# Final RMSNorm of a two-layer kernel: norm weight before the turn, token factor after it

## What is computed

```
def per_layer_embed(h, p_i, norm_w, w_gate, w_proj):
    gate = jax.nn.sigmoid(rmsnorm(h, norm_w) @ w_gate)
    return ((p_i @ w_proj) * gate).astype(h.dtype)
...
        h = h + per_layer_embed(h, p[i], ple_norm_w[i], ple_w_gate[i], ple_w_proj[i])
    return rmsnorm(h, final_norm_w)
```

## Time and profile before

| | |
|---|---|
| runs shown | 1607.35, 1607.68, 1607.53 us |
| the profiled execution's own time | 1606.47 us |
| its span in the trace | 1604.8 us |
| TensorE (PE) matmul busy | 1524.5 us, 95% of the span |
| VectorE (DVE) busy | 1189.6 us, 74% |
| ScalarE (ACT) busy | 718.6 us, 45% |
| mean granted TensorE clock | 0.967 |

### The profile page before, as it was taken

The page is one execution under the profiler, slowest core; times in us unless marked ns, Lnnn a source line. Parts: engine busy times, 40 slices in busy tenths (PEclk is TensorE's granted clock), DMA queues, the critical chain, the costliest instruction groups (busy, mean ns, idle before and its releaser), DMA issues.

```text
span 1604.8 us, 20223 instructions
## 1 busy us (share of the span) xinstructions
PE 1524.5 (95%) x7365; PEld 1239.3 (77%) x7365; DVE 1189.6 (74%) x1371; ACT 718.6 (45%) x1091; POOL 243.8 (15%) x244
## 2 busy tenths in 40 slices
PE   7988999999989999999999989999999999999996
PEld 6757777687667888888876769988888888888884
DVE  5687768678787989988898969955677666643356
ACT  4554454444644555134445342433365555532242
POOL 1154111020127400030075100000100000000000
PEclk9999999999999999999999976979999999999998
DMA  4334215144225334543436587932233333332221
GB/s 141 86 122 132 79 66 173 51 145 131 66 66 108 115 119 143 196 133 130 151 118 209 174 299 249 264 85 94 93 95 99 94 93 103 105 98 92 92 92 59
DMA packets 192234, 199.01 MB, mean 124 GB/s; under 512 B 47886, under 2 KB 178526, under 8 KB 188062
## 3 DMA queue, kind: packets, MB, share of 16 engines
q1 hardware_dynamic: 184510, 192.76, 37.8%
q10 hardware_dynamic: 7648, 5.25, 1.2%
HBM read 169.47 MB, written 28.51 MB: 123 GB/s over the span
## 4 chain that ended last, share of the span: by engine, by line
PE 74%; DVE 15%; issue 5%; DMA 3%; ACT 2%; SPq 1%; POOL 0%; DVEq 0%; ACTq 0%
PE ring L2093 21%; PE ring L2083 21%; PE ring L2084 21%; DVE w_lo L1462 2%; PE ring L2349 2%; PE pe_s L2369 2%; DVE cc L1584 1%; PE ring L2234 1%; PE pe_s L2359 1%; DMA w_raw<-in_ssd_w_out 1%; DVE ytmp L1758 1%; DVE zs L1764 1%; DVE fwd L1622 1%; PE pe_s L2104 1%; DVE rstd L1486 1%
## 5 line engine op out<-in xcount | busy, mean ns | idle before, releaser
L2083 PE MATMUL ring<-uh,w_hi 128*128 128x512 f32 x1160 | 459.4, 396 | 10.5 <-DVE cc L1584 3.7
L2084 PE MATMUL ring<-ul,w_hi 128*128 128x512 f32 x1160 | 454.5, 392 | 0.0
L1045 ACT ACTIVATE w_hi<-w_raw 128x1024 fp32r<-128x1024 f32 (+1 forms) x233 | 239.5, 1028 | 437.5 <-PE ring L2084 348.4
L1462 DVE TENSOR_TENSOR w_lo<-w_raw,w_hi 128x1024 fp32r<-128x1024 f32 (+1 forms) x233 | 287.7, 1235 | 162.1 <-PE ring L2093 143.9
L2093 PE MATMUL ring<-uh,w_lo 128*128 128x512 f32 x1160 | 289.1, 391 | 6.3 <-DVE w_lo L1462 6.2
L2083 PEld LDWEIGHTS ring<-uh,w_hi 128*128 128x128 f32 x1160 | 219.5, 189 | 63.1 <-issue 10.9
L2093 PEld LDWEIGHTS ring<-uh,w_lo 128*128 128x128 f32 x1160 | 218.2, 188 | 53.5 <-DVE w_lo L1462 7.5
L2084 PEld LDWEIGHTS ring<-ul,w_hi 128*128 128x128 f32 x1160 | 219.4, 189 | 47.5 <-issue 1.7
L2083 PE MATMUL ring<-gh,w_hi 128*128 128x512 f32 x480 | 189.0, 394 | 4.0 <-ACT w_hi L1045 2.7
L2084 PE MATMUL ring<-gl,w_hi 128*128 128x512 f32 x480 | 188.1, 392 | 0.0
L1971 DVE SCALAR_TENSOR_TENSOR cc<-cin,par,cc 128x512 f32<-128x512 f32 x176 | 129.5, 796 | 1.0 <-ACT cc L1396 1.0
(11 more groups left out here) (329 smaller groups left out, 2050.9 us busy)
## 6 DMA issues: line engine op xcount, KB each, us to landing
w_raw<-in_ffn_w_up SPq DMA_DIRECT2D x88, 512.0 KB, 3.5
w_raw<-in_ffn_w_down SPq DMA_DIRECT2D x40, 512.0 KB, 3.4
w_raw<-in_ssd_w_in SPq DMA_DIRECT2D x32, 512.0 KB, 4.2
s_tables<-tab SPq DMA_DIRECT2D x16, 1024.0 KB, 4.9
slot<-s_tables SPq DMA_DIRECT2D x16, 1024.0 KB, 7.8
fwd<-log_decays SPq DMA_DIRECT2D x16, 512.0 KB, 5.0
w_raw<-in_ssd_w_out SPq DMA_DIRECT2D x16, 512.0 KB, 3.5
w_raw<-in_ple_w_gate SPq DMA_DIRECT2D x16, 512.0 KB, 3.4
```

Source lines behind the costliest of these rows:

```text
L1045: act.activation(w_hi[u % 2][:, 0:n], w_raw[:, u % 2, 0:n], ACT.Copy).then_inc(hi_done, 1)
L1462: dve.tensor_tensor(w_lo[u % 2][:, 0:n], w_raw[:, u % 2, 0:n], w_hi[u % 2][:, 0:n].bitcast(F32), ALU.subtract).then_inc(lo_done, 1)
L2083: pe.matmul(o, wh[:, k, c], rh[:, k0 + k, :], start=first and k == 0, stop=False)
L2084: mm_ = pe.matmul(o, wh[:, k, c], rl[:, k0 + k, :], start=False, stop=False)
```

## The change

- The norm weight goes onto `h` before the statistics exist: `hn = h * weight`. ScalarE does tiles 0 to 5 right behind the square of each (`ACT.Identity` with a scale by partition), VectorE tiles 6 and 7 at the end (`tensor_scalar`).
- The left half (channels 0 to 511, tiles 0 to 3) of each of the four token blocks is turned during the last `ple` steps: `left_half(b)` on TensorE, four transposes into the free bank `pe_y`, and `left_half(b)` on ScalarE, a plain copy from `pe_y` into `o_sb`. Block 0 stands ahead of the projection product of i = 2, block 1 behind it, block 2 between the two gate products of i = 3, block 3 behind the second.
- The sums over the channels are taken with the squares as the stationary operand and one column of ones as the moving one, a matmul for each of four token blocks and three sources, 12 in all. The result is `pe_s[:, 0:4]`: tokens on the partitions. Variance, root and reciprocal (`token_var`, `token_rstd`) are 128x4.
- Since the tokens are then on the partitions in `o_sb` too, the factor is a scale by partition: VectorE multiplies the four left halves in place and takes the right half of block 1 from `ring`; ScalarE takes the right halves of blocks 0, 2 and 3 from `ring` (`ACT.Identity` with `t_rstd` as scale).
- At the end TensorE has 16 transposes (tiles 4 to 7), and they no longer wait for the statistics.
- The store of a block waits for its left and right half. `hn` and `o_sb` lie higher in SBUF.

```
--- before.py
+++ after.py
@@ -72,7 +72,7 @@
                 tile(("down", layer, part), 8, True)
             tile(("gate", layer, 0), 4, True)
             tile(("gate", layer, 1), 4, True)
-        tile("final", 8)
+        tile("final", 4)
 
         units = 0
         mixer = []
@@ -318,8 +318,11 @@
         ffn1 = ffn_memory(1, layer1)
         layer1.close()
         last = ExitStack()
+        sb("below_last", [P, 2 * KD * SEQ], where=last)
         hn = sb("hn", [P, KD, SEQ], where=last)
         o_sb = sb("o_sb", [P, SB, D], where=last)
+        t_var = sb("token_var", [P, SB], where=last)
+        t_rstd = sb("token_rstd", [P, SB], where=last)
         last.close()
         UH, UL = [uh0, uh1], [ul0, ul1]
         FFN = [ffn0, ffn1]
@@ -787,7 +790,9 @@
 
             o_v = out[0].rearrange("(b p) d -> p b d", p=P)
             for b in range(SB):
-                sp.wait_ge(evac, T["final"] + 2 * b + 2)
+                if b != 1:
+                    sp.wait_ge(evac, T["final"] + (1, None, 2, 3)[b])
+                sp.wait_ge(hn_done, KD + (1, 3, 4, 5)[b])
                 sp.dma_start(o_v[:, b, :], o_sb[:, b, :]).then_inc(stored, 16)
             sp.wait_ge(stored, 16 * SB)
 
@@ -1242,6 +1247,11 @@
                     squares(1, m)
                     u_hi(1, m, uh0)
 
+
+            def left_half(b):
+
+                act.wait_ge(spare_full, KD + 2 + b + 1)
+                act.activation(o_sb[:, b, 0:SEQ], pe_y[:], ACT.Copy).then_inc(spare_taken, 1)
 
             for layer, parts in enumerate(PARTS):
                 gh, gl, p_in, ph, pl = FFN[layer]
@@ -1439,14 +1449,25 @@
                 std(r)
                 for i in range(4):
                     hi_to(u + GATE[i] + 3)
+                    if layer == 1 and i >= 2:
+                        left_half(2 * i - 4)
                     for m in (2 * i, 2 * i + 1):
                         act.wait_ge(evac, T[("gate", layer, m // 4)] + m % 4 + 1)
                         act.activation(cc[:, m % 4, :], cc[:, m % 4, :], ACT.Sigmoid).then_inc(g_sig, 1)
                     hi_to(min(u + GATE[i] + 4, u + 13))
+                    if layer == 1 and i >= 2:
+                        left_half(2 * i - 3)
                     for m in (2 * i, 2 * i + 1):
                         squares(r + 1, m)
-                if layer == 1:
-                    std(r + 1)
+                        if layer == 1 and i < 3:
+                            act.activation(hn[:, m, :], h[:, m, :], ACT.Identity, scale=col(C_FIN + m)).then_inc(hn_done, 1)
+
+            act.wait_ge(var_done, 6)
+            act.activation(t_var[:], t_var[:], ACT.Sqrt).then_inc(std_done, 1)
+            act.wait_ge(rstd_done, 6)
+            for b in (0, 2, 3):
+                act.wait_ge(filled, FILL["final"] + b + 1)
+                act.activation(o_sb[:, b, SEQ:], bank(T["final"] + b), ACT.Identity, scale=t_rstd[:, b:b + 1]).then_inc(evac, 1)
 
 
         @block.vector
@@ -2055,14 +2076,21 @@
                     assert layer or i < 2 or made[0] == 12 * NB
 
 
-            rstd_of(6)
-            for m in range(KD):
+            for m in range(KD - 2, KD):
                 dve.wait_ge(*h_ready(6, m))
-                dve.scalar_tensor_tensor(out=hn[:, m, :], in0=h[:, m, :], scalar=col(NORM_COL[6] + m), in1=rstd[:],
-                                         op0=ALU.mult, op1=ALU.mult).then_inc(hn_done, 1)
+                dve.tensor_scalar(hn[:, m, :], h[:, m, :], col(C_FIN + m), None, ALU.mult).then_inc(hn_done, 1)
+            dve.wait_ge(sq_used, 3 * 6)
+            dve.tensor_scalar(t_var[:], pe_s[:, 0:SB], 1.0 / D, EPS, ALU.mult, ALU.add).then_inc(var_done, 1)
+            dve.wait_ge(std_done, 6)
+            dve.reciprocal(t_rstd[:], t_var[:]).then_inc(rstd_done, 1)
+            dve.wait_ge(rstd_done, 6)
             for b in range(SB):
-                for half in range(2):
-                    take("final", 2 * b + half, o_sb[:, b, half * SEQ:(half + 1) * SEQ])
+                dve.wait_ge(spare_taken, KD + 2 + b + 1)
+                dve.tensor_scalar(o_sb[:, b, 0:SEQ], o_sb[:, b, 0:SEQ], t_rstd[:, b:b + 1], None, ALU.mult).then_inc(hn_done, 1)
+                if b == 1:
+                    dve.wait_ge(filled, FILL["final"] + b + 1)
+                    dve.tensor_scalar(o_sb[:, b, SEQ:], bank(T["final"] + b), t_rstd[:, b:b + 1], None, ALU.mult
+                                      ).then_inc(hn_done, 1)
 
 
         @block.tensor
@@ -2471,6 +2499,15 @@
                             mm_ = pe.matmul(pproj(j), wl[:, k, c], ph[:, k, :], start=False, stop=k == PK - 1)
                     mm_.then_inc(unit_done, 1)
 
+                def left_half(b):
+
+                    pe.wait_ge(hn_done, 4)
+                    if b:
+                        pe.wait_ge(spare_taken, KD + 2 + b)
+                    for k in range(4):
+                        mm_ = pe.transpose(pe_y[:, k * P:(k + 1) * P], hn[:, k, b * P:(b + 1) * P], eye[:])
+                    mm_.then_inc(spare_full, 1)
+
                 pe.wait_ge(p_lo, PK * (layer + 1))
                 proj_product(0)
                 for i in range(4):
@@ -2483,23 +2520,31 @@
                         if (i, kg) == (0, 0):
                             add_square(r + 1, KD - 2)
                             add_square(r + 1, KD - 1)
+                        if layer == 1 and (i == 3 or (i, kg) == (2, 1)):
+                            left_half(0 if i == 2 else 2 + kg)
                     if i:
                         proj_product(i)
-                    if i:
-                        add_square(r + 2, 2 * i - 2)
-                        add_square(r + 2, 2 * i - 1)
-                add_square(r + 2, KD - 2)
-                add_square(r + 2, KD - 1)
-
+                    if (layer, i) == (1, 2):
+                        left_half(1)
+                if layer == 0:
+                    add_square(r + 2, KD - 2)
+                    add_square(r + 2, KD - 1)
+
+            for n, src in enumerate((var[:], sq[:, (KD - 2) % 2, :], sq[:, (KD - 1) % 2, :])):
+                if n == 0:
+                    pe.wait_ge(sq_add, ADDS * 6)
+                else:
+                    pe.wait_ge(sq_done, KD * 5 + KD - 2 + n)
+                for b in range(SB):
+                    mm_ = pe.matmul(pe_s[:, b:b + 1], src[:, b * P:(b + 1) * P], ones[:, 0:1], start=(n, b) == (0, 0),
+                                    stop=n == 2, skip_group_check=True)
+                mm_.then_inc(sq_used, 1)
+            pe.wait_ge(hn_done, KD)
+            pe.wait_ge(evac, T["final"])
             for b in range(SB):
-                for half in range(2):
-                    if b == 0:
-                        pe.wait_ge(hn_done, 4 * half + 4)
-                    pe.wait_ge(evac, T["final"] + 2 * b + half - 3)
-                    for k in range(4):
-                        mm_ = pe.transpose(bank(T["final"] + 2 * b + half)[:, k * P:(k + 1) * P],
-                                           hn[:, 4 * half + k, b * P:(b + 1) * P], eye[:])
-                    mm_.then_inc(filled, 1)
+                for k in range(4):
+                    mm_ = pe.transpose(bank(T["final"] + b)[:, k * P:(k + 1) * P], hn[:, 4 + k, b * P:(b + 1) * P], eye[:])
+                mm_.then_inc(filled, 1)
 
 
 # ---- launch: one core; inputs and outputs as the reference has them ----
```

## The result

The changed kernel took 1596.61 us (median of 5 runs, 1594.96 to 1599.84); the kernel before, beside it, 1607.53 us (1604.58 to 1608.59). The ratio is 0.9927, 95% interval 0.9909 to 0.9945, estimated from all the runs; the plain quotient of the two medians is 0.9932. The profiled execution took 1595.06 us, its span is 1593.3 us.

What follows compares the result with a forecast made beforehand. TensorE is 95% busy, but the exposed chain at the end was the target: last store 1601.7 to 1589.3, less 2.3 us given back to queued stores, saves 10.1 us from median 1607.53: 1597.4 us, range 1596.3 to 1600.4.

Steps and rivals of the forecast that it cites:

- the last term of the range: Low end of the forecast range: 0.3 us below 1596.6 us, allowed for the spread of the runs, giving 1596.3.
- The moved transposes: Sixteen transposes moved into the full product stream: TensorE pays 1.66 us, and everything behind them is that much later.
- The upper bound of 2.4: Moved transposes if each of four groups breaks the stream and drains once: 2.4 us in all, +0.8.
- ScalarE's place in the queue: Step i = 0: two weightings push the next `w_hi` unit from 1550.93 to 1552.3, still 0.4 us early; cost 0.
- The sums: One-column matmuls behind the last squares: 16 weight loads, 1.85 us, nothing won; at half price the end comes 0.4 us earlier.
- From the sums to the first store: Transposes and evacuation at the end: sums done at about 1586.3, first store issued at 1587.7.
- if the clock has held: Condition on the last 16 transposes, right behind the sums, costing 0.104 us each at full clock.
- The prediction's 0.4 us at most: Extra cost if, by the skill's rule, transposes do not count as activity that raises the clock.
- The stores: Four queued output stores: 0.84 us to first bytes, 5.16 us of bytes, 0.97 us to the end at 1594.7.
- The rival of slow queued stores: Queued output stores drain at 290 GB/s, 7.2 us for four: 2.0 us more, 1599.4 us; chance 0.10.
- the bound of about 358 GB/s: Memory-side limit for a core on the final stores: the four would take 5.9 us, 0.7 more.
- the other rivals: Stream disturbed, 1 to 3 us (0.13); gain within 3.2 us of no change (0.04); clock falls, 11 us slower (0.03).

Runs made afterwards that it cites:

- the longer comparison: The changed kernel against the kernel before, both without an edit, on another occasion: 11 runs against 16, ratio 0.9948 (0.9929 to 0.9966).
- columns_twice: Changed kernel with the one-column matmuls of the last two squares issued twice; end 53.9 us from the last stage's first gate product, 3.3 more than the changed kernel.
- gap_filled3: Changed kernel plus seven wide matmuls ahead of TensorE's wait for the square of tile 6; end 50.21 and 50.25 us from the last stage's first gate product.
- two_stores3: Changed kernel without the stores of token blocks 2 and 3; span 1601.1 us, end 47.9 us from the last stage's first gate product.

## Why the prediction was right and wrong

**The time.** The forecast was 1597.4 us, within 1596.3 to 1600.4, and the median is 1596.61. But the measured ratio, 0.9927, puts the changed kernel at 1607.53 x 0.9927 = 1595.8 us beside that kernel before, half a microsecond under the low end (its interval reaches from 1592.9 to 1598.7). The step that failed is the last term of the range: "below, 0.3 us go to the spread of the runs". I had three runs within 0.33 us and took that for the spread. Later runs of the kernel before range over 14 us, and its five of the first occasion over 4 us; the mark moves by 11 us with the same code. The gain itself is 9.4 us by the mark, and 8.4 us by the longer comparison (1607.53 x (1 - 0.9948)); both are less than the forecast of 10.1. By the longer comparison the time would be 1599.2 us, inside the range. So the chain was forecast 0.7 us too well, the first runs came out some 2 us better than the chain explains, and that the median lies so near the forecast is partly luck.

**The moved transposes** were mis-sized: 1.66 us by the term, 1.95 measured. Sixteen in a row was the wrong row, since four groups break the stream four times. The first product matmul behind a group starts its successor after 0.32 us instead of 0.23:

```profile
1570.65 0.60 PE L2508 MATMUL pe_y<-eye,hn 128*128 128x128 f32 x4
1571.00 0.48 PE L2111 MATMUL ring<-uh,w_hi 128*128 128x512 f32 x1
1571.32 0.39 PE L2112 MATMUL ring<-ul,w_hi 128*128 128x512 f32 x1
```

Four times 0.09 us is 0.36, about the 0.3 that the term lacked; this is an estimate from one group. The upper bound of 2.4 held.

**ScalarE's place in the queue** was right: the `w_hi` unit that two weightings delay was to be done 0.4 us ahead of its use by the working; it was done at 1549.99 and used at 1550.63, 0.6 us later, and TensorE shows no gap. VectorE waited 0.62 us for it, which nothing waited for:

```profile
1550.02 1.23 DVE L1483 TENSOR_TENSOR w_lo<-w_raw,w_hi 128x1024 fp32r<-128x1024 f32 x1 [0.62 <-ACT w_hi L1050]
```

**The sums** were right: "nothing is won in this step", 1.85 us by the term, 2.02 and 1.95 measured, and `columns_twice` shows that they are paid in full. The table load ended at 1584.42, 0.2 us ahead of them, and the root started at 1584.83; faster sums could bring the statistics forward by no more than these 0.4 us, as the bound said.

**From the sums to the first store** I had 1.4 us; it was 1.8 and 1.6. This is the second step that failed, and the largest part of the miss on the chain: the condition "if the clock has held" stood in the sum without a price, and it was not met. I had read the fall of the clock in the earlier trace rows as a thing of idle time alone and counted the one-column sums as work that holds it. The prediction's 0.4 us at most, given there for another reason, was the right size, and `gap_filled3` gives the 1.4 us when the clock holds.

The rule of the Trainium skill cited on this ("TensorE: Matmul & The Clock Gate", section on PE-mode transpose, that transposes do not count as activity that raises the clock) is spoken against again: in the changed kernel the clock rose between 1587.5 and 1588 with nothing but transposes since 1584.46. The sum was right to reject that reason and still lost the 0.4 us, by a clock that fell behind the idle gap and over the one-column sums.

**The stores** were right: first issue to end 6.97 us by the working, 6.93 and 6.94 measured, bytes without a gap. The rival of slow queued stores (290 GB/s) falls, and the bound of about 358 GB/s that the prediction took from the Trainium skill, page "DMA: Bandwidth & Descriptors" (section Bandwidth), did not bind: 2.1 MB in 5.2 us are 400 GB/s. The same section gives that figure also as the share of a core whose neighbour on the same memory streams too, and this program runs on one core. `two_stores3` shows that they set the end.

The sum by terms, from the mark: forecast 49.94 us, measured 50.63. Of the 0.7 us, 0.3 are the moved transposes, 0.1 the sums and 0.4 the fallen clock, less 0.1 at the stores. None of the other rivals came: no stall of the stream, no clock below 1.0 between the mark and 1580.

## What to carry to other kernels

A normalization at the end of a program is a chain of engines that wait for each other. What does not need the statistics (weight, turning, copies) can go ahead of them, and with rows on partitions the statistics shrink from 512 columns to 4 and the factor becomes a scale at evacuation. Ask then what bounds the end: here it became the 5.2 us of output bytes, after which an earlier first store helps, or fewer bytes. And before a range is made from a few runs that agree, take the distance from a mark just ahead of the change; it repeated within 0.3 us in two profiles of each kernel, where the whole time varied by 10.

## What was not expected of the hardware

- One-column fp32 matmuls let the clock fall to 0.50 although TensorE was busy in every window: 80 records (40 matmuls) took 13.77 us. Their price goes with the clock, 0.11 us a record at 1.00 and 0.21 at 0.50.
- The time of the same code up to the mark varied from 1542.7 to 1553.9 us over twelve profiles, and longer runs had the lower mean clock (0.975 at 1602.66 us, 0.964 at 1616.85).
- A store of 512 KB cut in two halves with rows of 2 KB cost the end some 0.1 us: from the first store to the end were 7.08 us instead of 6.96.
